# GpSimd forms suffix sums for the stick-breaking heads, and TensorE's products with minus ones shrink

## The reference

```python
def one_block(args):
    i, q_blk = args
    z = jnp.einsum('bhqd,bhkd->bhqk', q_blk, kt).astype(jnp.float32) * scale
    q_pos = i * BLOCK + jnp.arange(BLOCK)
    causal = key_pos[None, :] < q_pos[:, None]
    log_one_minus = jnp.where(causal, jax.nn.log_sigmoid(-z), 0.0)
    suffix = lax.cumsum(log_one_minus, axis=3, reverse=True) - log_one_minus
    log_a = jax.nn.log_sigmoid(z) + suffix
    a = jnp.where(causal, jnp.exp(log_a), 0.0)
    return jnp.einsum('bhqk,bhkd->bhqd', a.astype(vt.dtype), vt)
```

## Time and profile before

| quantity | value |
|---|---|
| runs before (3) | 1914.83, 1915.09, 1916.83 us |
| profiled execution | 1917.37 us, span 1915.6 us |
| TensorE busy | 1897.8 us, 99% of the span |
| VectorE, ScalarE, GpSimd busy | 964.2, 772.1, 182.8 us |
| chain that ended last | PE 88%, ACT 5%, DVE 5% |
| stretch of the stick-breaking heads | about 1347.7 to 1434 us of the span |

### The profile page before, as it was taken

How to read it: one execution, slowest core, us unless ns; L and a number is a source line. 1 busy time by engine, 2 the same in 40 slices (tenths; PEclk the granted TensorE clock), 3 DMA queues, 4 the chain that set the end, 5 groups by cost and what they waited for, 6 DMA issues and landing times.

```text
span 1915.6 us, 25105 instructions
## 1 busy us (share of the span) xinstructions
PE 1897.8 (99%) x10458; PEld 1567.2 (82%) x10458; DVE 964.2 (50%) x1497; ACT 772.1 (40%) x1251; POOL 182.8 (10%) x196
## 2 busy tenths in 40 slices
PE   9999999999999999999999999999999999999998
PEld 7878888888888867888888888878887888888887
DVE  5693665553245284566553236443655555425523
ACT  5494433333333295433333334233764443212321
POOL 4112200000005031300000103000000020000000
PEclk9999999999999999999999999999999999999999
DMA  6512233334333311232233332331112323233222
GB/s 191 197 35 77 80 97 99 99 92 141 93 104 123 99 41 56 89 98 92 97 99 91 102 105 99 99 106 61 59 38 86 116 90 97 99 99 96 93 97 88
DMA packets 54136, 182.96 MB, mean 96 GB/s; under 512 B 6604, under 2 KB 10060, under 8 KB 53512
## 3 DMA queue, kind: packets, MB, share of 16 engines
q1 hardware_dynamic: 51528, 172.28, 28.2%
q0 software_dynamic: 2352, 9.02, 1.6%
q10 hardware_dynamic: 144, 0.06, 0.0%
HBM read 176.58 MB, written 4.76 MB: 95 GB/s over the span
## 4 chain that ended last, share of the span: by engine, by line
PE 88%; ACT 5%; DVE 5%; issue 1%; DMA 1%; SPq 0%; DVEq 0%; ACTq 0%
PE bank L1903 22%; PE bank L1904 22%; PE bank L1905 22%; PE bank L1922 2%; ACT prob_long L848 2%; PE bank L1923 2%; PE bank L1924 2%; ACT pt_short L837 1%; PE bank L2153 1%; PE bank L1683 1%; PE bank L1686 1%; PE bank L1691 1%; PE bank L1981 1%; PE bank L1982 1%; PE bank L1983 1%
## 5 line engine op out<-in xcount | busy, mean ns | idle before, releaser
L1155 DVE TENSOR_TENSOR w_lo<-w_raw,w_hi 128x1024 fp32r<-128x1024 f32 (+3 forms) x319 | 388.6, 1220 | 712.3 <-ACT w_hi L661 711.9
L661 ACT CAST w_hi<-w_raw 128x1024 fp32r<-128x1024 f32 (+3 forms) x319 | 322.0, 1010 | 555.0 <-DMA w_raw<-in_w_down 132.4
L1903 PE MATMUL bank<-h_hi,w_hi 128*128 128x512 f32 x1272 | 497.1, 391 | 0.8 <-DVE w_lo L1155 0.5
L1904 PE MATMUL bank<-h_lo,w_hi 128*128 128x512 f32 x1272 | 496.1, 390 | 0.0
L1905 PE MATMUL bank<-h_hi,w_lo 128*128 128x512 f32 x1272 | 495.9, 390 | 0.0
L1903 PEld LDWEIGHTS bank<-h_hi,w_hi 128*128 128x128 f32 x1272 | 239.5, 188 | 53.1 <-issue 2.2
L1905 PEld LDWEIGHTS bank<-h_hi,w_lo 128*128 128x128 f32 x1272 | 239.5, 188 | 50.2
L1904 PEld LDWEIGHTS bank<-h_lo,w_hi 128*128 128x128 f32 x1272 | 239.5, 188 | 49.5
L1903 PE MATMUL bank<-a_hi,w_hi 128*128 128x512 f32 (+1 forms) x676 | 261.5, 387 | 0.0
L1904 PE MATMUL bank<-a_lo,w_hi 128*128 128x512 f32 (+1 forms) x676 | 261.3, 387 | 0.0
L1905 PE MATMUL bank<-a_hi,w_lo 128*128 128x512 f32 (+1 forms) x676 | 261.3, 386 | 0.0
(11 more groups left out here) (328 smaller groups left out, 2551.6 us busy)
## 6 DMA issues: line engine op xcount, KB each, us to landing
w_raw<-in_w_gu SPq DMA_DIRECT2D x87, 512.0 KB, 3.5
w_raw<-in_w_mlp_in SPq DMA_DIRECT2D x32, 512.0 KB, 3.5
w_raw<-in_w_mlp_out SPq DMA_DIRECT2D x32, 512.0 KB, 3.6
w_raw<-in_w_down SPq DMA_DIRECT2D x32, 448.0 KB, 3.3
w_raw<-in_w_out SPq DMA_DIRECT2D x24, 512.0 KB, 3.6
w_raw<-in_w_down SPq DMA_DIRECT2D x16, 512.0 KB, 3.5
w_raw<-in_w_gates SPq DMA_DIRECT2D x16, 512.0 KB, 3.4
w_raw<-in_w_qk_b SPq DMA_DIRECT2D x14, 512.0 KB, 3.7
```

The costliest lines, as they stand in the source:

```text
L661: nc.scalar.copy(hi_of(v), raw_of(v)).then_inc(w_hi_done, 1)
L1155: nc.vector.tensor_tensor(lo_of(v), raw_of(v), hi_of(v).bitcast(F32), ALU.subtract).then_inc(w_split, 1)
L1903: mm(acc, w1, hi, start=start, stop=False)
L1904: mm(acc, w1, lo, start=False, stop=False)
```

## The change

Products with minus ones over several later key tiles apply the same matrix to several pieces of L and add the results. The changed kernel adds the pieces first. For head s, GpSimd waits for `l_ready`, then adds in place in L tile 3's 128 columns to the last 128 of tile 2, then the 256 columns of tile 2 to the last 256 of tile 1. These two sums, 384 columns, are split in `tail_hi` and `tail_lo` by two casts and two subtractions. The last subtraction brings `tails_ready` to 2s + 2. TensorE, in the block of head e, runs the two `neg_tri` products of tile 0 and then waits for `tails_ready` 2e + 2. Its products with `neg_ones` take the next tile's first 128 columns from `L_hi`/`L_lo` and all further columns from the tails. That is 128 + 256, 128 + 128 and 128 columns in each of the two parts: 768 columns in 5 products, where it was 384 + 256 + 128, 256 + 128 and 128: 1280 columns in 6 products. ScalarE's wait before it overwrites L two heads later is on `tails_ready` instead of `l_ready`. `sb_key` moves by 512 bytes.

```diff
@@ GpSimd, between biases(2) and sum_streamed(10)
+            def sum_tails(s):
+
+                L = prob[:, s % 2, :]
+                pool.wait_ge(l_ready, s + 1)
+                nc.gpsimd.tensor_tensor(L[:, 1152:1280], L[:, 1152:1280], L[:, 896:1024], ALU.add).then_inc(tails_added, 1)
+                pool.wait_ge(tails_added, 2 * s + 1)
+                nc.gpsimd.tensor_tensor(L[:, 640:896], L[:, 640:896], L[:, 1024:1280], ALU.add).then_inc(tails_added, 1)
+                for i, (src, dst) in enumerate(TAILS):
+                    pool.wait_ge(tails_added, 2 * s + 2)
+                    nc.gpsimd.tensor_copy(tail_hi[:, dst], L[:, src]).then_inc(tails_hi, 1)
+                for i, (src, dst) in enumerate(TAILS):
+                    pool.wait_ge(tails_hi, 2 * s + i + 1)
+                    nc.gpsimd.tensor_tensor(tail_lo[:, dst], L[:, src], tail_hi[:, dst].bitcast(F32),
+                                            ALU.subtract).then_inc(tails_ready, 1)
@@ ScalarE
-                        act.wait_ge(l_ready, s - 1)
+                        act.wait_ge(tails_ready, 2 * (s - 1))
@@ TensorE, block of sums of head e, for each key tile kt
-                            for later in range(kt + 1, 4):
-                                w = S - P * later
-                                first = col + P * (later - kt)
-                                src = STICK[later][2]
-                                for part in (L_hi, L_lo):
-                                    last = mm(z[b][:, first:first + w], neg_ones[:, :], part[:, src:src + w],
-                                              start=False, stop=later == 3 and part is L_lo, skip_group_check=True)
+                            if kt == 3:
+                                continue
+                            pe.wait_ge(tails_ready, 2 * e + 2)
+                            at_, far = STICK[kt + 1][2], TAILS[kt][1] if kt < 2 else slice(0, 0)
+                            for part, tail in ((L_hi, tail_hi), (L_lo, tail_lo)):
+                                last = mm(z[b][:, col + P:col + 2 * P], neg_ones[:, :], part[:, at_:at_ + P],
+                                          start=False, stop=kt == 2 and part is L_lo, skip_group_check=True)
+                                if kt < 2:
+                                    last = mm(z[b][:, col + 2 * P:col + S - P * kt], neg_ones[:, :], tail[:, far],
+                                              start=False, stop=part is L_lo, skip_group_check=True)
```

More of the change, by code:

```diff
@@ L161, in program @@
         ident_r = place("ident_r", [P, P], F32R, low + 26 * K)
-        sb_key = place("sb_key", [P, S], F32, low + 29 * K)
+        tail_hi = place("tail_hi", [P, 384], F32R, low + 26 * K + 512)
+        tail_lo = place("tail_lo", [P, 384], F32R, low + 28 * K)
+        sb_key = place("sb_key", [P, S], F32, low + 29 * K + 512)
         memT = place("memT", [P, DC, MEM], F32, high + 20 * K)
@@ L268, in program @@
         l_hi_done, l_ready, masks_rounded = sem("l_hi_done"), sem("l_ready"), sem("masks_rounded")
+        tails_added, tails_hi, tails_ready = sem("tails_added"), sem("tails_hi"), sem("tails_ready")
         l_set, c_ready, a_exp = sem("l_set"), sem("c_ready"), sem("a_exp")
@@ L461, in program @@
         STICK_BANKS = [(0, 512), (512, 512), (1024, 256)]
+        TAILS = ((slice(640, 896), slice(0, 256)), (slice(1152, 1280), slice(256, 384)))
         block = ctx.enter_context(nc.Block())
@@ L642, in _ @@
             biases(2)
+            def sum_tails(s):
[11 more added lines that the diff above has]
+                                            ALU.subtract).then_inc(tails_ready, 1)
+            for s in range(N_SB):
+                sum_tails(s)
             sum_streamed(10)
```

## The result

The changed kernel takes 1924.48 us, the median of 5 runs (1923.34 to 1927.95), against 1915.09 us (5 runs, 1913.92 to 1916.83). The ratio is 1.005, with a 95% interval of 1.0039 to 1.0061: slower by 9.4 us. Forecast were 1923.1 us and a range of 1916.5 to 1927.0.

The account below looks back on a forecast made before the run. TensorE, busy in 1897.8 of 1915.6 us, was taken as the bound. Waits of 4.4 + 3.2 + 0.2 us, less 2.8 saved, plus 3.05 for the clock make +8.05 on 1915.09: 1923.1 us, range 1916.5 to 1927.0.

Parts of the forecast that it names:

- What TensorE saves: Products with minus ones in the heads' blocks: 0.35 us less a head, 2.8 us for 8 heads.
- The chain alone: GpSimd's six instructions for each head, with hand-overs, take 3.5 us when VectorE does not disturb them.
- The chain beside VectorE: GpSimd's instructions stand while VectorE reads two SBUF operands: chain of 6.1 us at head 0, 3.8 at head 7.
- The waits: TensorE stands for the tails 4.4 us at head 0, 3.2 at head 7, 0.2 on three odd heads together.
- The other edits: TensorE's later waits, ScalarE's wait and GpSimd's slowing of VectorE: put at nothing.
- The clock: TensorE's clock falls to half once, most likely at head 0's wait, costing 3.05 us.
- The rival with two falls: The clock falls at heads 0 and 7, giving 1926.2 us; chance 0.15.

Follow-up runs that it names:

- the narrow products alone: The changed kernel without GpSimd's chain and its waits, far columns reading L_hi and L_lo: 1912.63 us.
- hold_vector: The changed kernel, but at head 0 VectorE waits for the tails before its two w_lo and the remainders: 1923.16 us.
- chain_only: The changed kernel with the wide products of before and TensorE's one wait on the tails moved behind the last head: 1916.0 us.
- late_wait: The changed kernel with a block's 14 products that need no tail ahead of the wait, four behind it: 1919.59 us.
- fill_head0: The changed kernel with 17 products of 512 columns, never read, ahead of TensorE's wait at head 0: 1920.44 us.
- inner_heads: The changed kernel with tails for heads 1 to 6 only; heads 0 and 7 keep the block of the kernel before: 1913.69 us.
- late_filled: The late_wait kernel with its waits at heads 0 and 7 filled by 11 and 6 unread products of 512 columns: 1916.3 us.

## Why the prediction was right

- *What TensorE saves, 2.8 us.* Right in its sum: 0.36 a block, 2.9 in all, and 2.5 alone. Wrong in one detail: the narrow product's extra cost appears in the step of the product behind it. The Trainium skill (TensorE: Matmul & The Clock Gate, section Back-to-back issue gap) has about 81 ns for a sustained product of 128 columns, which as an estimate makes 3.4 us; the blocks, 2.9 us shorter in all, and the 2.5 us of the narrow products alone disagree.
- *The chain alone, 3.5 us.* It took 3.2 in hold_vector. The add of 128 columns was put at 0.46 and measured at 0.46; the hand-overs were sized a little too high.
- *The chain beside VectorE, 6.1 us at head 0 and 3.8 at head 7.* Measured 5.7 and 3.6. Walking the two engines in turn gave the right size from one row. That an operand in a bank costs nothing was an assumption; the adds at head 7, at 0.46 and 0.73 us beside such instructions, bear it out. The Trainium skill (GPSIMD Engine Reference, section Specifications) has the two engines share their way to SBUF when VectorE has two SBUF inputs; the adds at head 0 and 7 and the held VectorE agree with it.
- *The waits, 4.4 and 3.2 us, and 0.2 on the odd heads.* Measured 4.1, 3.0 and 0.5. The odd heads' 0.5 came from heads 3 and 5 alone, with 0.25 each.
- *The other edits, nothing.* GpSimd's load on VectorE cost 0.8 us without any wait on the tails (chain_only). In the change TensorE has no wait on the gate bank in the stage: it is hidden by the waits on the tails.
- *The clock, one fall of 3.05 us.* There were two, at 2.7 and 1.7 us. The rival with two falls, given 0.15, is what the profile shows, but with a smaller price each: 4.4 in sum, where I had put two at 6.1, and 1.3 more than one fall as I sized it. The waits less the saving came to 4.7 us where I had 5.0. So the stage's 9.1 us are 1.05 above my 8.05, and the median lies 1.4 us above the forecast.

So the mechanism was right in its waits and its saving, and in part wrong in the clock. That the time still came so near owes something to luck: the case that came true had its own number, 1926.2, and its falls were cheaper than I priced them. The term worth most doubt was the clock, and its condition was misjudged: I took 2.9 us of little work as near the least that matters. It fell at waits of 2.53 and 1.44 us as well (late_wait), and it held at waits of 1.38, 1.92 and 0.80 us (hold_vector). So the length of a wait did not settle by itself whether the clock fell, and what did was not shown.

## What to carry to other kernels

Where one engine bounds the kernel, do not ask whether a helper engine has time, but how long it is from its input to its output at each hand-over, and compare that with the slack at the tightest one. Here six of eight places had nearly all the cover that they needed, one of them (head 1) only because head 0's wait made TensorE late, and two had not; the two cost 7.1 us of waiting where all eight together saved 2.9. Leave out the ends of such a loop, place the wait behind everything that does not need the result, and compare stages rather than spans where an execution's clock varies. Here that took away the loss; that it leaves a gain over the kernel before is not shown.

## What was not expected of the hardware

- In one execution a pause of TensorE of 1.44 us was followed by 3.4 us at 1.2 GHz, and one of 2.53 us by 6.8 us. In another, pauses of 1.38 and 1.92 us were followed by none. The same pauses as in the first, filled with products whose results nobody reads, left the clock at 2.4 GHz and gave 3.3 us back.
- An add of 128 columns on GpSimd took 0.46 us, or 1.37 us when it met VectorE's two-operand instruction of 1024 columns. VectorE was slowed as well: the w_lo pair took 2.62 us instead of 2.35, and the sb_ks behind it 1.10 instead of 0.69.
- The fall of the clock at the one-column products lasted 6.8 us in the profiled execution before and 3.4 in the one after, with the same instructions, and was absent in three others (fill_head0, inner_heads, late_filled). As an estimate, half of 6.8 us, that alone moves a span by up to some 3 us.
